# A float32 decoder block on one core: input and memory also loaded in turned layout, and the first product fed with rows whose scale is applied later

## What is computed

```python
def rms_norm(x, w):
    xf = x.astype(jnp.float32)
    y = xf * lax.rsqrt(jnp.mean(xf * xf, axis=-1, keepdims=True) + NORM_EPS)
    return (y * w).astype(x.dtype)
...
    p = xn @ w_in                                    # 1024 x 3072, xn = rms_norm(x, attn_norm_w)
    p_rwkv, p_swa, p_mem = jnp.split(p, [RWKV_PROJ, RWKV_PROJ + SWA_PROJ], axis=-1)
...
    km, vm = jnp.split(mem_n @ w_mem_kv, 2, axis=-1) # mem_n = rms_norm(mem, mem_norm_w)
...
    h = h + sparse_moe(rms_norm(h, ffn_norm_w[l]), ...)   # 32 experts, 12 MB of weights each
```

## Time and profile before

| | us |
|---|---|
| three timed runs: median 1276.69 | 1276.27, 1276.69, 3164.12 |
| the profiled execution | 1278.25 |
| its span (first to last recorded instruction) | 1276.5 |

### The profile page before, as it was taken

One profiled execution on the slowest core, in us unless ns is written; L12 is line 12 of the kernel. 1 busy time (PEld: TensorE's weight loads), 2 busy tenths in 40 slices (PEclk: granted clock), 3 DMA queues, 4 the chain that ended last, 5 costly groups with the idle time before them and its releaser, 6 DMA issues.

```text
span 1276.5 us, 15523 instructions
## 1 busy us (share of the span) xinstructions
PE 1209.3 (95%) x6554; PEld 594.2 (47%) x6554; DVE 371.0 (29%) x634; ACT 184.0 (14%) x355; POOL 0.2 (0%) x4
## 2 busy tenths in 40 slices
PE   8999999999999999999999999989899898989896
PEld 7887777888544343333333333232323233232322
DVE  2058452411133223133222323222231312322223
ACT  2234621300121010110101010010101011000102
POOL 0000000000000000000000000000000000000000
PEclk9999999999999999999999999999999999999999
DMA  9344212597489999999999999999999999999995
GB/s 350 119 156 149 67 35 68 178 391 317 156 301 407 427 429 427 428 427 428 427 427 428 429 430 428 428 428 428 428 431 428 428 427 428 428 429 429 429 426 239
DMA packets 52710, 448.74 MB, mean 352 GB/s; under 512 B 5649, under 2 KB 18065, under 8 KB 27058
## 3 DMA queue, kind: packets, MB, share of 16 engines
q1 hardware_dynamic: 52272, 447.10, 85.1%
q10 hardware_dynamic: 386, 0.92, 0.2%
HBM read 446.96 MB, written 1.05 MB: 351 GB/s over the span
## 4 chain that ended last, share of the span: by engine, by line
PE 70%; DMA 25%; DVE 4%; issue 1%; ACT 0%; SPq 0%; PEldq 0%; DVEq 0%
PE ps L535 67%; DMA ring<-in_w_exp 18%; DMA upper<-in_w_exp 6%; PE ps L1087 1%; DVE ring L1561 1%; DMA xrows<-in_x 0%; PE ps L796 0%; DVE ring L1664 0%; PE ps L1096 0%; DVE upper L1938 0%; DVE upper L1645 0%; DVE ring L1558 0%; PE ps L702 0%; DVE upper L1600 0%; ACT upper L1271 0%
## 5 line engine op out<-in xcount | busy, mean ns | idle before, releaser
L535 PE MATMUL ps<-ring,upper 128*64 128x512 f32 (+4 forms) x2656 | 508.4, 526 | 29.8 <-DMA ring<-in_w_exp 18.9
L535 PE MATMUL ps<-upper 128*64 128x512 f32 (+5 forms) x1844 | 329.3, 461 | 17.0 <-DMA upper<-in_w_exp 11.8
L535 PEld LDWEIGHTS ps<-ring,upper 128*64 128x64 f32 (+2 forms) x2656 | 164.2, 136 | 340.4 <-issue 292.7
L535 PEld LDWEIGHTS ps<-upper 128*64 128x64 f32 (+3 forms) x1844 | 154.0, 154 | 174.0 <-issue 143.8
L535 PE MATMUL ps<-xT,ring 128*128 128x256 f32 x672 | 150.5, 381 | 0.4 <-DVE xT L1522 0.4
L535 PEld LDWEIGHTS ps<-xT,ring 128*128 128x128 f32 x672 | 126.1, 190 | 18.7 <-issue 1.8
L1854 DVE TENSOR_TENSOR xrows<-xrows,ps 128x1024 f32<-128x1024 f32 x30 | 36.5, 1216 | 268.0 <-PE ps L535 250.5
L1833 DVE TENSOR_TENSOR upper<-ps,merged 128x512 f32<-128x512 f32 x32 | 22.1, 692 | 229.9 <-PEq L1059 216.2
L1421 ACT ACTIVATE xT<-upper 128x512 f32<-128x512 f32 x32 | 20.2, 632 | 374.2 <-DVE upper L1836 374.1
L1427 ACT ACTIVATE factors<-ps 64x512 f32<-64x512 f32 x63 | 37.3, 591 | 246.5 <-PEq L1082 245.8
L535 PE MATMUL ps<-factors,cst 128*128 128x512 f32 x128 | 62.9, 615 | 3.8 <-PE ps L535 2.8
(11 more groups left out here) (234 smaller groups left out, 506.5 us busy)
## 6 DMA issues: line engine op xcount, KB each, us to landing
ring<-in_w_exp SPq DMA_DIRECT2D x120, 2048.0 KB, 34.7
upper<-in_w_exp SPq DMA_DIRECT2D x63, 2048.0 KB, 34.4
ring<-in_w_exp SPq DMA_DIRECT2D x13, 1024.0 KB, 8.1
ring<-in_w_gate SPq DMA_DIRECT2D x9, 1024.0 KB, 5.2
ring<-in_w_in SPq DMA_DIRECT2D x8, 896.0 KB, 12.1
ring<-in_w_in SPq DMA_DIRECT2D x8, 640.0 KB, 3.9
ring<-in_w_branch SPq DMA_DIRECT2D x5, 1024.0 KB, 5.1
ring<-in_w_mem_kv SPq DMA_DIRECT2D x4, 1024.0 KB, 4.9
```

The source lines that it names most:

```text
L535: return pe.matmul(o, l, r, start=start, stop=stop, skip_group_check=True)
```

## The change

- `x` is given a second time, turned (`x_turned`, columns on partitions). It is loaded straight into `xT`: chunks 0 and 1 by a transfer that ACT issues, chunks 2 to 7 by one of SP behind n0. `mem` is given a second time as well, and goes straight into `memT`, behind n3.
- The rows of `x` are still loaded, for their sums of squares and for later use, but behind n1, and `ident` behind them. `prm` is issued by ACT.
- DVE multiplies `xT` in place by the column factors. The first product takes this `xT`, without the tokens' factors.
- The tokens' factors are needed along the free axis on all partitions. DVE makes a diagonal matrix of them (`diagonal`), PE multiplies it with a tile of ones (`spread_scale`, in PSUM bank 7, behind chunk 1 for `x` and behind chunk 3 for `mem`), and DVE copies the result to `row_scale`.
- DVE, not ACT, takes the first product's seven banks from PSUM, and multiplies by `row_scale` there. For the second product and the gates it multiplies `xT` itself in place (`row_scaled(c)`), once PE's first product has used chunk `c`.
- For the memory, one DVE instruction a chunk multiplies the turned tile by both factors.
- Gone: 16 transposes of `x` and 16 of `mem` on PE, the scaling of rows and the eviction of `xT` on DVE, and on ACT the seven copies of the first product and the eight of `memT`. `keep_awake` runs 5 matmuls on ones in place of 6 on zeros.

On the engine side the diff reads (cut):

```diff
-            sp.dma_start(xrows[:, 0, :], x[0, 0:P, :]).then_inc(x_loaded[0], 16)
-            sp.dma_start(cst[:, 0:P], consts[:, 0:P]).then_inc(ident_loaded, 16)
-            sp.dma_start(xrows[:, 1, :], x[0, P:T, :]).then_inc(x_loaded[1], 16)
-            sp.dma_start(prm[:], params).then_inc(prm_loaded, 16)
...
+                if n == 0:
+                    sp.dma_start(xT_flat[:, XT_FIRST * T:], x_turned[:, XT_FIRST * T:]).then_inc(xT_full, 16)
+                if n == 1:
+                    for t in range(TT):
+                        sp.dma_start(xrows[:, t, :], x[0, t * P:(t + 1) * P, :]).then_inc(x_loaded[t], 16)
+                    sp.dma_start(cst[:, 0:P], consts[:, 0:P]).then_inc(ident_loaded, 16)
...
+                    sp.dma_start(memT.rearrange("p c t -> p (c t)"), mem_turned).then_inc(mem_loaded, 16)
...
-            keep_awake(6, 7, zeros)
...
+            keep_awake(5, 7, unit)
+            def spread_scale(k):
+                pe.wait_ge(scaled, TT * (k + 1))
+                if k:
+                    pe.wait_ge(xT_sb, KC + 1)
+                mm(half(7, 0), unit[:, 0:P], scales[:, k, :]).then_inc(row_ps, 1)
             for c in range(KC):
                 w = take("in_rwkv", c)
+                pe.wait_ge(xT_sb, c + 1)
...
+                if c in (1, 3):
+                    spread_scale(c // 2)
...
+            act.dma_start(xT_flat[:, 0:XT_FIRST * T], x_turned[:, 0:XT_FIRST * T]).then_inc(xT_first, 16)
+            act.dma_start(prm[:], params).then_inc(prm_loaded, 16)
...
-            act.wait_ge(mem_loaded, 16)
+            act.wait_ge(mem_loaded, 32)
...
+            dve.wait_ge(prm_loaded, 16)
+            for c in range(KC):
+                if c == 0 or c == XT_FIRST:
+                    dve.wait_ge(xT_full if c else xT_first, 16)
+                TS(xT[:, c, :], xT[:, c, :], col("attn", c), None, ALU.mult).then_inc(xT_sb, 1)
+            dve.wait_ge(ident_loaded, 16)
...
+            def row_scaled(c):
+                dve.wait_ge(xT_sb, c + 1)
+                dve.wait_ge(slots_used, min(c + 1, KC - 1))
+                if c == KC - 1:
+                    dve.wait_ge(rwkv_ps, 7)
+                TTn(xT[:, c, :], xT[:, c, :], row_scale[:, 0, :], ALU.mult).then_inc(xT_sb, 1)
...
+            dve.wait_ge(row_ps, 2)
+            link(dve.tensor_copy(row_scale[:, 1, :], ps[:, 7, 0:T]))
+            dve.wait_ge(mem_loaded, 32)
+            for k in range(KC):
+                STT(memT[:, k, :], memT[:, k, :], col("memn", k), row_scale[:, 1, :], ALU.mult, ALU.mult).then_inc(memT_sb, 1)
+            for c in range(3, KC - 1):
+                row_scaled(c)
+            for b in range(7):
+                dve.wait_ge(rwkv_ps, b + 1)
+                TTn(raw[:, 2 * b:2 * b + 2, 1:T + 1], ps[:, b, :].rearrange("p (c t) -> p c t", c=2),
+                    row_scale[:, 0, :].unsqueeze(1).to_broadcast([P, 2, T]), ALU.mult).then_inc(raw_sb, 1)
```

More of the change, by code:

```diff
@@ L116 @@
 N_FILL = 8
+XT_FIRST = 2
 def fill_points():
@@ L604, in low_rank @@
                     last.then_inc(kk_ps, 1)
[L605 to L616, removed]
             for c in range(KC):
                 w = take("in_rest", c)
+                pe.wait_ge(xT_sb, KC + c + 1)
                 for f in range(10):
@@ L1211, in _ @@
             act.wait_ge(act_step, 4)
-            act.activation(ss[:, 6:8], ss[:, 2:4], ACT.Sqrt, scale=1.0 / D, bias=epsc[:, 0:1]).then_inc(root_m, 1)
-            for b in range(7):
-                act.wait_ge(rwkv_ps, b + 1)
-                act.activation(raw[:, 2 * b:2 * b + 2, 1:T + 1], ps[:, b, :].rearrange("p (c t) -> p c t", c=2), ACT.Copy).then_inc(raw_sb, 1)
+            act.activation(ss[:, 6:8], ss[:, 2:4], ACT.Sqrt, scale=1.0 / D, bias=epsc[:, 0:1]).then_inc(root, 1)
             act.wait_ge(lora_in, 1)
@@ L1236, in _ @@
             act.activation(ss[:, 7:8], epsc[:, 0:1], ACT.Exp)
-            for n in range(2):
-                act.wait_ge(memT_ps, n + 1)
-                for i in range(4):
-                    bank = 7 - i // 2 * 2 if n == 0 else 6 + i // 2
-                    act.activation(memT[:, 4 * n + i, :], ps[:, bank, (i % 2) * T:(i % 2 + 1) * T], ACT.Copy,
-                                   scale=col("memn", 4 * n + i)).then_inc(memT_sb, 1)
             act.wait_ge(csum_sb, 1)
@@ L1514, in _ @@
                 link(dve.reciprocal(ss[:, 4 + t:5 + t], ss[:, 4 + t:5 + t]))
-                TS(xscaled[:, t, :], xrows[:, t, :], ss[:, 4 + t:5 + t], None, ALU.mult).then_inc(scaled, 1)
-            dve.wait_ge(prm_loaded, 16)
+                diagonal(0, t, ss[:, 4 + t:5 + t])
             step(TS(omka[:], prm[:, PCOLS["ka"]:PCOLS["ka"] + 4], -1.0, 1.0, ALU.mult, ALU.add))
             TS(bq[:], prm[:, PCOLS["bswa"]:PCOLS["bswa"] + 4], SWA_SCALE, None, ALU.mult)
-            for c in range(KC):
-                if c % 2 == 0:
-                    dve.wait_ge(xT_ps, c // 2 + 1)
-                TS(xT[:, c, :], ps[:, c // 2, (c % 2) * T:(c % 2 + 1) * T], col("attn", c), None, ALU.mult).then_inc(xT_sb, 1)
-            dve.wait_ge(root_m, 1)
+            dve.wait_ge(row_ps, 1)
+            link(dve.tensor_copy(row_scale[:, 0, :], ps[:, 7, 0:T]))
+            row_scaled(0)
+            row_scaled(1)
+            dve.wait_ge(root, TT + 1)
             link(dve.reciprocal(ss[:, 6:8], ss[:, 6:8]))
             for t in range(TT):
-                TS(memrows[:, t, :], memrows[:, t, :], ss[:, 6 + t:7 + t], None, ALU.mult).then_inc(scaled_m, 1)
-            link(dve.memset(raw[:, :, 0:1], 0.0))
+                diagonal(1, t, ss[:, 6 + t:7 + t])
+            row_scaled(2)
+            step(dve.memset(raw[:, :, 0:1], 0.0))
+            dve.wait_ge(row_ps, 2)
[9 more added lines that the diff above has]
+                    row_scale[:, 0, :].unsqueeze(1).to_broadcast([P, 2, T]), ALU.mult).then_inc(raw_sb, 1)
+            settle()
             def shift(a, b, signal):
@@ L1537, in _ @@
             shift(12, 14, lora_in)
+            row_scaled(KC - 1)
             shift(0, 12, shifted)
@@ L1965 @@
     arrays["in_consts"] = constants()
+    for name in ("x", "mem"):
+        turned = np.asarray(inputs[name])[0].T.reshape(KC, P, -1).transpose(1, 0, 2)
+        arrays[f"in_{name}_turned"] = np.ascontiguousarray(turned.reshape(P, -1))
     args = [nc.dram_tensor(name, a.shape, F32, kind="ExternalInput").ap() for name, a in arrays.items()]
```

27 lines of the change are left out of this document (12 added, 15 removed).

## The result

The changed kernel is slower: 1279.81 us (median of 13 runs, 1279.33 to 1281.07) against 1276.89 for the kernel before (13 runs). The ratio is 1.0025, with a 95% interval of 1.0018 to 1.0033, so 2.3 to 4.2 us. The forecast was 3.3 us faster, with a range up to 1277.0. The loss is small, but it is real and outside the range. One of the 13 runs of the kernel before took 3164.12 us; the ratio is taken over the fast runs, without it.

A forecast was written before the change was run, and what follows sets the result against it. A gapless weight-transfer stream bounds the kernel, its start set by PE's progress, so front shifts reach the end. Earlier start 4.2 less added matmuls 0.87 gives 3.3 us (cap 3.6): 1276.69 - 3.3 = 1273.4 us, range 1271.0 to 1277.0.

The forecast's parts named there:

- the clamp: Start of the instruction behind `kk_ps`, L1548 before and L1568 after: forecast at 85.1 us in place of 88.4.
- The start of the product: PE's first real matmul: at about 7.2 us in place of 11.38, released by n0, 4.2 us won.
- the first rival: At the front, small transfers queue behind large ones: PE starts at 10.2, gain 0.3 us, time 1276.4; chance 0.12.
- The clock: Rival: shorter keep-awake and a gap leave the product's first matmuls at 1.2 GHz, each us so spent losing half.
- the form that decides: Clock rival, chunk 0 and more at 1.2 GHz, 10 us: loses 5 us, 1278.4, slower than before; chance 0.04.
- the short form of the clock: Clock rival, three us of the product's start at the lower level: loses 1.5 us, 1274.9; chance 0.18.
- The base: Product start of 11.38 from the profiled execution of before; the runs' median, 1276.69, lies 1.56 us below that execution.
- The two matmuls: Two `spread_scale` matmuls of 256 columns added on PE's path in the first product: 0.434 us each, 0.87 in all.
- n4: Weight transfer for chunk 4 of the first product: lands at 32.1, wanted at 32.4, caps the gain at 3.6 us.
- The memory's transposes: 16 on PE after `kk_ps`, 2 x 1.04 us, beside DVE's chain: removal gains nothing; rival gain 5.4, chance 0.06.
- the longer PE wait ahead of the transposes of `probs`: Sign expected in the profile after: PE waits longer there, at about 114.5 us.
- its two assumptions: At the product's start: small transfers land before n0, so PE starts at about 7.2; its matmuls run at full pace.

The follow-up runs named there:

- spread x5: The kernel with one queue and 8 keep-awake matmuls, with each of the two `spread_scale` matmuls issued five times: 1278.51 us, ratio to before 1.0015.

## Why the prediction was wrong, step by step

The forecast had the clamp 3.3 us earlier than before; it came 3.6 to 3.8 us later than in the usual execution of before (90.68 and 90.75 against 87.07 and 86.96). The difference of 7.0 us has three parts, each of which a run isolates:

- **The start of the product, 2.8 us.** The sentence that failed is "They are small and issued first [...] so I take the lower side, before 6.7, which makes n0 the last." n0's own landing, put at 7.1, was close (7.34). Nor were they issued first: SP issued n0 and the turned rest at the same 0.74 and 1.20. The small transfers shared the engines with SP's queue and the second of them landed at 9.5, as in the first rival ("PE starts at 10.2"). Swapping them and putting them on one queue showed both halves of this. The rule of the Trainium skill, page "DMA: Bandwidth & Descriptors" (Queues, rings and completion order), that an engine goes round its queues a packet at a time, was read too hopefully: going round does not serve the small transfer first. The trace agrees with taking turns (221 packets against 207 by 7.6 us), but equal turns in packets were 1.39 MB against 0.28, so a transfer with few bytes in as many packets was done no sooner than the large one at its side.
- **The clock, 2.9 us.** It stood as a rival with 0.18 for 1.5 us and 0.04 for the form that decides. I priced its probability from a gap of one us, because the start was put at 7.2. But the rivals were not independent: late `prm` makes the gap four us long, and the gap brings down the clock. As priced there, on a start of 11.38 for before, neither the late transfer nor the short form of the clock alone ends on the slow side; together they do, and the two chances should not have been treated apart. The run with 14 keep-awake matmuls gives the price, 80.71 - 77.82 = 2.89. In the run with the small transfers swapped it was not the gap but the short keep-awake that left the clock low, so the shortened keep-awake that the prediction named counts too; the two traces of the changed kernel itself both show the fall. By the Trainium skill's page "TensorE: Matmul & The Clock Gate" (What's actually happening) the slow level is the default and activity lifts it. The traces agree, with the fall to 0.50 in the idle gap and with the slow transposes of the kernel with one keep-awake matmul.
- **The base, 1.3 to 1.4 us.** The start of 11.38 belonged to an execution 1.56 us above the median. The prediction noted the 1.56 and then subtracted it as if it lay evenly over the kernel. It sat in exactly the stage that the change replaces: the second half of `x` landed 1.3 to 1.5 us later than in the three other traces. The prediction put the slow stretch from 5 to 6 us (220 GB/s) down to the narrow rows of `ident` and `prm`. The two further traces have the same transfers there, at 330 and 417 GB/s, so the rows are not what made it. The change therefore had 2.8 us to win at the start, not 4.2, and the prediction's own sum on the usual start is 2.8 - 0.87 = 1.9 us.

By sums: the start is level (9.91 to 10.04 against 9.94 to 10.05), two matmuls cost 0.87, half pace costs 2.9, and 3.8 us is what the clamp should lose; it lost 3.6 to 3.8. The timed runs lost 2.9. The remaining 0.7 to 0.9 us lies within what single executions differ behind the clamp (up to 1.3), and no run resolves it.

**What held.** The shift at the clamp reached the end of the kernel in every run. The two matmuls cost their full time (spread x5). The memory's transposes were covered (kept: no change). PE showed no wait ahead of the clamp other than the first one in the changed kernel, so DVE's evictions and row scaling, the memory's factors and n4 were all in time: DVE's seven evictions took 692 ns each with 0.17 us to spare between them. n4 landed at 30.3 in the changed kernel against 32.1 forecast (its base of 27.1, too, was later than the 24.8 to 26.8 of the three other traces of before), and became visible as the next bound (0.3 us) once the start was at 6.48. One sign named in advance did not appear: the longer PE wait ahead of the transposes of `probs`. The time went into a wait for ACT (L1241) some 13 us earlier, at no cost.

With its two assumptions made true by edits, the change is worth 1.9 us (8 keep-awake matmuls on one queue), and 3.0 us with n0 in halves.

## What to carry to other kernels

When a change brings forward the first use of an engine, list every transfer that this use waits for and put them on one queue in the order of need, ahead of the large ones; a small transfer that is second on its own queue lands with the large one that is second on the other. Fill TensorE's idle time up to the real start, and size the filler by the measured landing, and by the executions in which the clock comes up late (how much to spare, no run shows): here one queue brought the kernel level with before, and three more cheap matmuls brought 1.9 us on top. Take more than one execution before using a start or a landing as the base of a sum of a few us, above all where the profiled execution is above the median, and ask whether two rivals would set each other off.

## What the runs showed of the hardware that was not expected

- Two queues with work: transfers issued at 0.74 on each landed together (7.34 and 7.54; 5.9 and 6.1 with the small ones swapped), and so did those issued at 1.2 (9.3 and 9.5; 8.5 and 8.9), although they carried from 40 to 896 KB. By 7.6 us the queues of the changed kernel had sent 221 and 207 packets, and 1.39 and 0.28 MB.
- The row of the granted clock begins at 1.00 whatever PE does: the ten keep-awake records of the changed kernel from 1.25 us on take 0.45 us each at a clock of 1.00, and in the run with the small transfers swapped four us of the product show the pace of 1.2 GHz (11 records in 4 us) beside a clock of 1.00:

```profile
10.00:14.00 4.00, 4.00 (x11) 1.00 1.04 416
```

In the changed kernel and on one queue the clock had first risen and then fallen, and the row shows the 0.50. The pace of the records is the safer witness.
- The same work brings the clock up at different times. In the two executions of one kernel (one queue, 8 keep-awake matmuls, PE busy from 1.25 us on) the pace doubled between 5 and 6 us in one (6 records in that us) and at about 7 in the other (still 4 records from 6 to 7).
- The same first 1 MB of transfers lands 1.3 to 1.5 us apart from one execution to the next: the rate at 5 to 6 us was 220 GB/s in the earlier trace rows, and 330 and 417 in the second and third trace of the same kernel.
